# The four weight sums of a head, made by accumulating DMAs on the GpSimd queue instead of VectorE additions

## The reference, cut to what matters

```python
q, k, v, g = jnp.split(xn @ w_in, [h * dk, 2 * h * dk, 2 * h * dk + h * dv], axis=-1)
scores = jnp.einsum('bnihd,bnjhd->bnhij', qc, kc) * inner_decay
y_inner = jnp.einsum('bnhij,bnjhv->bnihv', scores, vc)      # and a recurrent part across chunks
y = ((y - mu) * lax.rsqrt(var + GN_EPS)).reshape(b, s, h * dv)
return (jax.nn.silu(g) * y) @ w_out                          # added to the residual h
```

## Time and profile before

| | |
|---|---|
| median of 3 runs | 1553.36 us (1551.82 to 1553.9) |
| the profiled execution | 1553.85 us, of which the span from first to last instruction is 1551.6 us |
| PE busy | 1531.0 us, 99% of the span, 6788 matmuls |
| DVE busy | 1153.2 us, 74% |
| ACT busy | 926.6 us, 60% |
| POOL busy | 4.6 us |
| DMA | 318.42 MB, 205 GB/s; queue q1 takes 60.9% of the 16 DMA engines' time |
| HBM read | 297.40 MB |

### The profile page before, as it was taken

One profiled execution on the slowest core, in us unless ns is written; L12 is line 12 of the kernel. 1 busy time (PEld: TensorE's weight loads), 2 busy tenths in 40 slices (PEclk: granted clock), 3 DMA queues, 4 the chain that ended last, 5 costly groups with the idle time before them and its releaser, 6 DMA issues.

```text
span 1551.6 us, 19968 instructions
## 1 busy us (share of the span) xinstructions
PE 1531.0 (99%) x6788; PEld 1259.3 (81%) x6788; DVE 1153.2 (74%) x1418; ACT 926.6 (60%) x1108; POOL 4.6 (0%) x12
## 2 busy tenths in 40 slices
PE   9999999999999999999999999999999999999997
PEld 7777878888887888888888888888888888888885
DVE  6989888888979888997766675775577557755665
ACT  7466574747566474756767556644664476446843
POOL 0000000000000000000000000000000000000000
PEclk9999999999999999999999999999999999999998
DMA  9485665757666565765566657655765576555651
GB/s 383 162 255 181 208 200 186 203 174 232 202 215 187 181 201 193 217 212 200 194 206 228 199 208 210 224 197 196 222 213 200 189 216 219 216 204 186 219 195 74
DMA packets 133498, 318.42 MB, mean 205 GB/s; under 512 B 80545, under 2 KB 80561, under 8 KB 112337
## 3 DMA queue, kind: packets, MB, share of 16 engines
q1 hardware_dynamic: 132608, 314.35, 60.9%
q0 software_dynamic: 704, 3.27, 0.5%
q10 hardware_dynamic: 144, 0.26, 0.0%
HBM read 297.40 MB, written 2.10 MB: 193 GB/s over the span
## 4 chain that ended last, share of the span: by engine, by line
PE 75%; DVE 10%; issue 6%; ACT 4%; DMA 4%; SPq 1%; ACTq 0%; DVEq 0%
PE accA L493 9%; PE accA L494 9%; PE accA L495 9%; PE accC L493 9%; PE accC L494 8%; PE accC L495 8%; PE accB L493 5%; PE accB L494 5%; PE accB L495 5%; DVE w_lo L1232 3%; DMA halvesT_e<-halves_e 2%; DMA w_raw<-in_stream_dram 2%; ACT w_hi L850 1%; ACT words_e L929 1%; DVE t_raw L1237 1%
## 5 line engine op out<-in xcount | busy, mean ns | idle before, releaser
L1311 DVE TENSOR_TENSOR w_lo<-w_raw,w_hi 128x1024 fp32r<-128x1024 f32 x326 | 395.8, 1222 | 227.8 <-ACT w_hi L839 226.0
L839 ACT CAST w_hi<-w_raw 128x1024 fp32r<-128x1024 f32 x326 | 340.0, 1052 | 267.9 <-PE accA L495 100.7
L850 ACT CAST w_hi<-w_raw 128x1024 fp32r<-128x1024 f32 (+1 forms) x224 | 219.5, 998 | 166.2 <-PE accC L495 50.5
L1232 DVE TENSOR_TENSOR w_lo<-w_raw,w_hi 128x1024 fp32r<-128x1024 f32 (+1 forms) x224 | 255.4, 1152 | 61.1 <-ACT w_hi L850 60.4
L493 PE MATMUL accA<-w_hi,xa_hi 128*128 128x512 f32 x452 | 176.2, 390 | 1.0 <-DVE w_lo L1311 0.6
L495 PE MATMUL accA<-w_hi,xa_lo 128*128 128x512 f32 x452 | 175.9, 389 | 0.0
L494 PE MATMUL accA<-w_lo,xa_hi 128*128 128x512 f32 x452 | 175.9, 389 | 0.0
L493 PE MATMUL accC<-w_hi,xa_hi 128*128 128x512 f32 x396 | 155.0, 391 | 0.5 <-DVE w_lo L1232 0.2
L494 PE MATMUL accC<-w_lo,xa_hi 128*128 128x512 f32 x396 | 154.2, 389 | 0.0
L495 PE MATMUL accC<-w_hi,xa_lo 128*128 128x512 f32 x396 | 154.1, 389 | 0.0
L493 PEld LDWEIGHTS accA<-w_hi,xa_hi 128*128 128x128 f32 x452 | 84.8, 188 | 19.7 <-DVE w_lo L1232 1.1
(11 more groups left out here) (277 smaller groups left out, 2947.4 us busy)
## 6 DMA issues: line engine op xcount, KB each, us to landing
w_raw<-in_stream_dram SPq DMA_DIRECT2D x162, 1024.0 KB, 4.8
w_raw<-in_stream_dram SPq DMA_DIRECT2D x224, 512.0 KB, 4.9
h<-in_x_dram SPq DMA_DIRECT2D x4, 512.0 KB, 13.3
xT_raw<-in_xT_dram SPq DMA_DIRECT2D x3, 512.0 KB, 14.4
dec<-in_decay_dram POOLq DMA_DIRECT2D x1, 1024.0 KB, 9.2
fgain<-in_final_gain_dram POOLq DMA_DIRECT2D x1, 1024.0 KB, 7.1
out_dram<-emb SPq DMA_DIRECT2D x1, 1024.0 KB, 3.8
halvesT_e<-halves_e SPq DMA_TRANSPOSE x56, 6.1
```

Of the source, the lines that this page charges most:

```text
L839: act.copy(w_hi[:, r % RING, :], w_raw[:, r // 2, (r % 2) * 1024:(r % 2 + 1) * 1024]).then_inc(hi_ready, 1)
L850: act.copy(dst, unit_raw(name)).then_inc(hi_ready, 1)
L1232: dve.tensor_tensor(w_lo[:, u % RING, 0:n], unit_raw(ORDER[u]), w_hi[:, u % RING, 0:n].bitcast(F32), ALU.subtract).then_inc(lo_ready, 1)
L1311: dve.tensor_tensor(w_lo[:, r % RING, :], w_raw[:, r // 2, (r % 2) * 1024:(r % 2 + 1) * 1024], w_hi[:, r % RING, :].bitcast(F32), ALU.subt ...
```

## The change

The four sums are no longer made by DVE. A new POOL function `head_sums` issues eight DMAs a head that add a block from HBM onto the landing slot of X1 or X2 (`accum_op=ALU.add`), after DVE has finished the last unit that reads the old value. X1a holds X1, then X1+X2, X1+X2+X3, and all four; X2a holds X2, then X2+X3; the same with b. X2, X3 and X4 are thus read from HBM twice or more. ACT waits for the landing (`sum_landed`) in place of `t_ready`. `t1_raw`, `t3_raw` and the four sum functions are gone.

`ORDER` has M5a and M5b between M3a and M3b, and B5 between M2a and M2b. The slots of the loads are dealt out anew; the slots of X1 and X2 stay taken until M4 and M7. Several pieces of side work stand behind other unit numbers, and the q and k transposes stand ahead of load B4 instead of O2. A wait of ACT for M4b ahead of `v_hi`, and one for M7b ahead of `qkT_hi`, are gone.

```diff
-ORDER = ("h0 h1 h2 h3 A2 M1a A3 M1b A4 M3a A5 M3b A6 M5a A7 M5b "
-         "C4 M6a C5 M6b C6 M7a C7 M7b O0 M4a O1 M4b B4 M2a M2b O2 O3 O4 O5 O6 O7 B5 B6 B7").split()
+ORDER = ("h0 h1 h2 h3 A2 M1a A3 M1b A4 M3a A5 M5a A6 M5b A7 M3b "
+         "C4 M6a C5 M6b C6 M7a C7 M7b O0 M4a O1 M4b B4 M2a B5 M2b O2 O3 O4 O5 O6 O7 B6 B7").split()
...
-HEAD_LOADS = (("A0", 3, "h1"), ("A1", 0, "h3"), ("A2", 1, "A2"), ("X1a", 2, "M1b"), ("X2a", 3, "M3b"), ("A3", 4, "A3"), ("X1b", 5, "M3a"),
...
+HEAD_LOADS = (("A0", 3, "h1"), ("A1", 1, "h3"), ("A2", 2, "A2"), ("X1a", 0, "M4a"), ("A3", 3, "A3"), ("X1b", 4, "M4b"), ("A4", 5, "A4"),
...
-Y_TURN, QK_TURN = "C4", "O2"
-SUM_OF = {"M5": 0, "M6": 4, "M7": 2, "M4": 6}
+Y_TURN, QK_TURN = "C5", "B4"
+SUM_OF = {"M5": ("X1", 0), "M6": ("X1", 1), "M4": ("X1", 2), "M7": ("X2", 0)}
...
+            def add_block(hd, base, x, term, used):
+                n = names.index(term + x[2])
+                at = hd * (HEAD_U // (2 * RAW)) + ((RET1 - HEAD_U + n) // (2 * RAW))
+                pool.wait_ge(lo_ready, base + (AT[used] + 1))
+                pool.dma_start(slot(SLOT[x]), rounds[at, n // 2 % RAW, :, n % 2 * UNIT * COL:(n % 2 + 1) * UNIT * COL],
+                               accum_op=ALU.add).then_inc(sum_landed[x], 16)
+            def head_sums(hd, base):
+                add_block(hd, base, "X1a", "X2", "M1a")
+                add_block(hd, base, "X1b", "X2", "M1b")
+                pool.wait_ge(sum_landed["X1a"], hd * 48 - 32)
+                add_block(hd, base, "X1a", "X3", "M5a")
+                pool.wait_ge(sum_landed["X1b"], hd * 48 - 32)
+                add_block(hd, base, "X1b", "X3", "M5b")
+                wait_head_landed(pool, hd, "X2a")
+                add_block(hd, base, "X2a", "X3", "M1b")
+                wait_head_landed(pool, hd, "X2b")
+                add_block(hd, base, "X2b", "X3", "M1b")
+                pool.wait_ge(sum_landed["X1a"], hd * 48 - 16)
+                add_block(hd, base, "X1a", "X4", "M6a")
+                pool.wait_ge(sum_landed["X1b"], hd * 48 - 16)
+                add_block(hd, base, "X1b", "X4", "M6b")
...
                 if name[:2] in SUM_OF:
-                    act.wait_ge(t_ready, hd * SUMS + (SUM_OF[name[:2]] + "ab".index(name[2]) + 1 - SUMS))
+                    x, n = SUM_OF[name[:2]]
+                    each = 48 if x == "X1" else 16
+                    act.wait_ge(sum_landed[x + name[2]], hd * each + (n * 16 + 16 - each))
...
@@ ACT, head @@
-                    if u == 3:
+                    if u == 4:
                         g_sigmoid(hd - 1, base)
-                    if u == 6:
+                    if u == 8:
                         y_halves(hd - 1)
-                    if u == 14:
+                    if u == 19:
                         y_words(hd - 1)
-                    if u == 21:
+                    if u == 23:
                         qk_halves(hd)
-                    if u == 25:
+                    if u == 28:
                         qk_words(hd, base)
-                    if u == 30:
-                        act.wait_ge(lo_ready, base + (AT["M4b"] + 1))
+                    if u == 29:
                         act.wait_ge(c_fixed, hd * 2)
                         v_hi_part(hd, base + (AT["C7"] + 1))
@@ DVE, head @@
-                    if u == 4:
+                    if u == 6:
                         gate_y(hd - 1)
-                    if u in (6, 8):
-                        t1_sum(hd, (u - 6) // 2)
-                    if u in (10, 12):
-                        t3_sum(hd, (u - 10) // 2)
-                    if u in (14, 16):
-                        t2_sum(hd, (u - 14) // 2, base)
-                    if u in (22, 24):
-                        t4_sum(hd, (u - 22) // 2, base)
-                    if u == 21:
+                    if u == 23:
                         y_lo_part(hd - 1, False)
-                    if u in (18, 19):
-                        rotate(hd, base + (AT["A7"] + 1), hd * 3 - 1, (u - 18,))
-                    if u == 26:
+                    if u in (17, 19):
+                        rotate(hd, base + (AT["A7"] + 1), hd * 3 - 1, ((u - 17) // 2,))
+                    if u == 20:
+                        rotated(hd * 3 - 1)
+                    if u == 31:
                         qkT_lo_part(hd, False)
-                    if u == 28:
+                    if u == 27:
                         fix_w(hd, base)
-                    if u == 29:
+                    if u == 28:
                         fix_c()
-                    if u == 31:
+                    if u == 30:
                         v_lo_part(hd)
```

More of the change, by code:

```diff
@@ L295, in trunk @@
         c_read = sem("c_read")
-        t_ready = sem("t_ready")
+        sum_landed = {x: sem(f"sum_landed_{x}") for x in ("X1a", "X1b", "X2a", "X2b")}
         snap_ready = sem("snap_ready")
@@ L347, in load_of @@
             if name[0] == "M":
-                return {"M1": "X1", "M3": "X3", "M2": "X4"}[name[:2]] + name[2]
+                return {"M1": "X1", "M5": "X1", "M6": "X1", "M4": "X1", "M7": "X2", "M3": "X3", "M2": "X4"}[name[:2]] + name[2]
             return name
@@ L466, in _ @@
         def _(pool):
+            rounds = stream.rearrange("(i s) p n -> i s p n", s=RAW)
+            names = [name for name, _slot, _last in HEAD_LOADS]
+            def add_block(hd, base, x, term, used):
[19 more added lines that the diff above has]
+                add_block(hd, base, "X1b", "X4", "M6b")
             pool.wait_ge(xT_landed[NC - 1], 16)
@@ L474, in _ @@
             pool.dma_start(p_raw, pT).then_inc(p_landed, 16)
+            for hd in range(1, HEADS):
+                head_sums(hd, hd * HEAD_S + (RET1 - HEAD_S))
             pool.wait_ge(yT_done, 1)
@@ L653, in head @@
                 a_unit(5, base)
+                product_part("M5a", base, side[1][:], f_hi[0], f_lo[0], True)
+                a_unit(6, base)
+                product_part("M5b", base, side[1][:], f_hi[0], f_lo[0], False)
+                a_unit(7, base)
                 product_part("M3b", base, acc["C"][0][:], f_hi[3], f_lo[3], False)
-                a_unit(6, base)
-                product_part("M5a", base, side[1][:], f_hi[0], f_lo[0], True)
-                a_unit(7, base)
-                product_part("M5b", base, side[1][:], f_hi[0], f_lo[0], False)
                 v_unit(4, base)
@@ L677, in head @@
                 product_part("M2a", base, acc["B"][0][:], *a12, False)
+                g_unit(5, base)
                 product_part("M2b", base, acc["B"][0][:], *a12, False)
@@ L952, in qk_words @@
                 act.wait_ge(words_ready, hd * 4)
-                act.wait_ge(lo_ready, base + (AT["M7b"] + 1))
                 for b in range(2):
@@ L1398, in rotate, with rotated @@
                 ins.then_inc(a_read, 1)
+                if len(tiles) == TT:
+                    rotated(a_reads)
+            def rotated(a_reads):
                 dve.wait_ge(a_read, a_reads)
```

28 lines of the change are left out of this document (1 added, 27 removed), and 8 rows, old and new, of the table HEAD_LOADS.

## The result

The changed kernel takes 1596.17 us (median of 4 runs, 1572.88 to 1613.02), the kernel before 1553.63 in the same session: ratio 1.0188, 95% interval 1.0126 to 1.0249. The prediction was 1549.5, with a range from 1543 to 1564: wrong in sign, and outside the range. The ratio and its interval compare the fast runs alone, of this kernel 1591.46 and 1572.88; the two medians as they stand are 2.7% apart. The profiled execution took 1600.88 us, with a span of 1599.0.

What follows compares the result with a forecast made beforehand. PE was taken to bound the loop, with almost no room. Of 11.9 us lost, 7.35 for a new chain and 0.7 in the first head would remain: 3.85 less, 1549.5 us, range 1543 to 1564.

Steps and rivals of the forecast that it cites:

- There is room, with longer queues at the upper end: DMA engines in the loop: eight additions cost 12.6 to 25 us a head, and the engines can take them.
- rival (b): Additions crowd the DMA engines, so transposes and load B4 come later; 1.2 us later gives 1557.9 us; chance 0.13.
- The share: Busy share of the DMA engines in a head: from 0.63 to between 0.77 and 0.91.
- the walk: The prediction's timing of one head, unit by unit, from PE's plan at 0.2267 us a matmul.
- rival (a): First additions land late; beyond 11.2 us each microsecond costs 7; 1562.1 us at 13, 1578.9 at 15.4; chance 0.20.
- The sums' chain: Additions ahead of M4 to M7: tightest window 11.2 us, later ones 14 to 18, landing taken as 9.2; costs nothing.
- The purse: All that the seven heads lose against PE's matmul time: 11.9 us, 3.0 in the first head, 1.5 in each other.
- rival (c): Nothing is late, the loop loses only 1.4 us: 1542.9 us; chance 0.15 with what lies toward it.
- The chain through B4: Load B4 behind q's and k's transposes makes M2a 0.15 and B5 0.75 us late; 1.05 a head with restarts.

Runs made afterwards that it cites:

- e1: Changed kernel with y's two transposes in heads 1 to 7 replaced by plain copies of the same bytes: 1556.17 us, ratio 1.0015.
- e2: Changed kernel without any of the eight additions of a head, the new order and slots alone: 1542.14 us, ratio 0.9929.
- e4: Changed kernel with y's transposes held until the first two additions landed, and the second pair until the transposes landed: 1588.43 us, ratio 1.0227.
- e5: DMAs alone, ten phases of additions, plain loads and transposes, run twice: two transposes landed after 3.3 and 3.1 us alone, 8.0 and 24.5 beside eight additions.
- e10: DMAs alone, six phases with whole and 128 KB additions: two transposes landed after 8.6 and 24.7 us beside 8 whole ones, 6.6 and 10.2 beside 32 quarters.
- e11: DMAs alone, forty phases, 1 or 4 additions and two transposes begun at steps of some 1 us: one addition took 5.3 to 5.6 us at every lag.
- e12: DMAs alone, additions issued 0.3 to 3 us behind two transposes in steps of some 0.2 us: at 1.20 us one addition took 9.6 in the repeat.
- e3: Changed kernel with plain loads on POOL's queue in place of the accumulating ones, sums not made: 1548.91 us, ratio 0.9974.
- e9: Changed kernel with each 512 KB addition issued as four of 128 KB: 1595.01 us, ratio 1.0276.
- e6: Kernel before, sums on DVE, B5's load and unit moved between M2a and M2b, load ahead of q's and k's transposes: 1563.53 us, ratio 1.0072.
- e8: e6 with q's and k's transposes issued ahead of load B5 again: 1545.68 us, ratio 0.9954 against the kernel before.

## Why the prediction was wrong

**The step that failed** is the one on the DMA engines, "There is room, with longer queues at the upper end", and with it rival (b), which let the crowding meet only q's and k's transposes and priced it at 1.2 us a head. The share was right (0.83 in the quiet heads, between 0.77 and 0.90 in all), but it says nothing of what stands beside what. y's transposes stand between the first pair of additions and the next, and in no line of the walk; rival (a) has transposes in flight beside an addition, but as a load on the addition and with no time of their own. In their place the runs show: beside additions y's transposes landed after up to 40.6 us instead of 6.8, additions after up to 41.4, and C5's load waits behind the transposes on SP's queue. The pair is the cause: without transposes there (e1) 33 to 40 us are gone, without the additions (e2) PE has no wait above 0.5 us left in the loop, and held apart (e4) the transposes land after 3.2 to 5.4.

How the pair does it is shown in part. Taking turns (e5, e10, e11) is shown for DMAs alone, but it can't be the whole price: in the quiet heads, where additions and transposes meet too, a head of 88.1 us loses 0.2, and the first head moves far fewer packets than turns would. What is added there looks like the crawl of e12, where the addition moves 9 to 16 packets in a microsecond from 34 to 39 us; that it is the same is argued, and why packets of both queues then take several times as long stays open. Whether it needs additions and long packets is open too: e3 and e9, which have no long stall, also moved the moment at which the queues meet.

The Trainium skill has the rule that I did not weigh: each engine goes round the queues that have work for it, a packet at a time (DMA: Bandwidth & Descriptors, Queues, rings and completion order). The turns of e5 agree with it, the first head's 40.6 us do not follow from it. Where that page of the Trainium skill lets an engine drain a packet of some 9 to 17 descriptors before it switches, the trace here differs: its records of 4 KB and 256 B move about one for one (815 and 743).

**The sums' chain** was right in what it called tightest and wrong in that it decides: the first additions had windows of 12.1 and 11.2 us and took 7.0 to 9.6, beside my 9.2. The later ones, "due" with 14 to 18 us, took up to 16.1 in a quiet head and 41.4 in the first. Rival (a) named late additions, but the first pair, which was in time, and at 1.8 us a head.

**The additions without y's transposes beside them** cost 14.0 us (e1 against e2), where I had nothing; plain loads in their place cost 6.8 (e3). PE stood 3.4, 5.9 and 2.4 us in three heads of e1, and ACT 58.0 before landings. The copies that e1 puts in place of the transposes have a part in that, and how much is not shown; that SP's loads take turns with the additions is the likely rest.

**The purse** was right: 11.9 us, and e2 has all of it. So was rival (c) as a price: 1542.9 forecast for "nothing is late", 1542.14 measured in e2, where no additions are in flight.

**The chain through B4**, 1.05 us a head, came in three heads of seven and small: 1.2 us in all, most in the third (0.24 ahead of M2a, 0.44 ahead of B5). (Its 0.15 at M2a is 0.07 by its own figures, 57.2 against 57.13, which hardly moves the sum.) I took SP's 3.72 us and a landing of 4.5 from before, where a load was issued 0.8 us ahead of the transposes. In the new order no load is so near: the two transposes took SP 2.54 us in e2 and landed after 2.7 to 2.8; in the change, with the last additions about, they landed after 2.7 to 4.7. e6 shows the same chain where it does exist, at 1.6 to 2.9 us a head.

**The rest**: HBM reads rose by 29.4 MB (29 forecast), the wait for `v_lo` went, POOL got its 56 issues. DVE's busy time fell by 56.7 us, not by 68.2. And from e8 to e2, which differ by DVE's sums and by the rest of the new order, is 3.5 us: unless the rest of the order hides a loss, the change removed work that held up nearly nothing.

## What to carry to other kernels

Before a stream of DMAs is put on a second queue, look for small-packet DMAs on the first one, transposes above all: the two queues take turns packet by packet, so each small packet waits for one of the other queue's for as long as that has any, whatever the mean share of the engines. Accumulating DMAs beside transposes can take far longer than that. Look then at what stands behind them on their own queue. Test an order apart from the mechanism that it came with: here the order, with DVE free of the sums, held all the gain, and the accumulating DMAs all the loss.

## What the runs showed of the hardware that I had not expected

- An accumulating DMA's 4 KB packet takes 327 ns, a plain one's 159 (about half the rate, as the Trainium skill, Collectives: The Full Stack, The bandwidth ceiling, has it for a reducing DMA); a 512 KB addition alone lands after 5.4 us (a plain one on the same queue 4.4), and behind others after 2.5 us more each.
- With DMAs alone, two queues move packets one for one, not byte for byte: two transposes of 3.2 us take 13.5 to 14.1 beside eight plain loads and up to 24.7 beside eight additions, but 5.5 to 5.8 among loads of their own queue.
- Beyond that there are lags at which an addition and transposes slow each other: 9.6 to 11.4 us for a first addition of 5.4, when it is alone and issued 1.20 us behind the first transpose (but not at 0.95 or 1.47) or 0.08 ahead of it (but not at 0.18). With three more additions it also comes at 0.9, and at 0.7 in one of two repeats. Why is open. In e5 it came with all compute engines idle, so none of them is needed for it. Plain copies of the same 256 B packets, at the place of the kernel's longest stall, landed after at most 12.1 us instead of 40.6.
- Behind a rest of 6.96 us PE's matmuls started 0.43 us apart, and so they did again behind the next rest of 20.24, until the clock came back near 149 us; the head lost some 4.7 us beside its waits.
